# Grouped heads: two weight parts split in a head's first slot, the output's low part right behind the rotation, and fewer small VectorE instructions

## The chip, the cores and the metric

The kernel runs on one core of one Trainium2 chip. The metric is the device time of one execution in microseconds, the median of three runs. Five engines work side by side and meet at semaphores: TensorE (PE, matrix products and transposes), VectorE (DVE), ScalarE (ACT), GpSimd (POOL) and SyncE (SP, which issues the transfers).

## The reference, cut to what matters

The program computes two transformer blocks one after the other on 512 tokens of width 1024. The change touches one stage of the first, the differential attention of eight heads:

```python
def rms_norm(x, g):
    y = x * lax.rsqrt(jnp.mean(x*x, axis=-1, keepdims=True) + NORM_EPS)
    return y * g

def diff_attention(h, cos, sin, w_qkv, q_norm, k_norm, lam_p, subln, w_o, layer_idx):
    q, k, v = jnp.split(h @ w_qkv, [DA_QK, 2 * DA_QK], axis=-1)
    q = apply_rope(rms_norm(q.reshape(B, S, DA_HEADS, 2, HEAD_DIM), q_norm), cos, sin)
    k = apply_rope(rms_norm(k.reshape(B, S, DA_HEADS, 2, HEAD_DIM), k_norm), cos, sin)
    ...
    def one_block(args):                      # one block of 128 queries
        s = jnp.einsum('bqhcd,bkhcd->bhcqk', qblk, k) * scale
        p = jax.nn.softmax(jnp.where(causal, s, NEG_INF), axis=-1)
        a = p[:, :, 0] - lam * p[:, :, 1]
        return jnp.einsum('bhqk,bkhe->bqhe', a, v)
    ...
    o = rms_norm(o, subln) * (1.0 - lambda_init)
    return o.reshape(B, S, DA_V) @ w_o
```

A head has two score maps of depth 64 and one value matrix of width 128. Its two softmaxes are subtracted, and the result of each head is normalised over its 128 features. The rest of both blocks (grouped and windowed attention, convolutions, gated feed-forward layers, norms) is not touched.

## The kernel before

Every large product is made in three parts from operands split into a high and a low part: `w_hi` and `w_lo` for the weights, `hx_hi` and `hx_lo` for the activations. ACT writes `w_hi` from the loaded `w_raw`, and DVE writes `w_lo` as the difference.

**The stage of the heads** (`heads` on each engine) runs 8 heads, and each head `h` has 4 slots `i`, one for each block of 128 queries. The instructions of every engine stand in a fixed order, written by hand in its function `slot`; a head of the middle is one half of a loop body. In a slot, PE does in this order: the scores of head `h`, block `i` (L1991, with the mask at L1995); the transposes of the probabilities of the block before (L2004); in slot 3 the transposes of the output of head `h-1` (L2018, `turn_outputs`); the projection of one token tile of head `h+1`, 24 matmuls (L1969 to L1971); the product of the block before with the values (L2011); and `turn_qk`, the transposes of a rotated tile (L1979), which wait for DVE's `rope` of that tile. In slot 3, `turn_qk` shares a PSUM bank with the output of head `h-1` and waits for DVE's `outputs_low(h-1)` as well. PE takes its instructions in order, so whatever `turn_qk` waits for holds back the next slot.

DVE does in a slot: two row maxima of the scores (L1577); in slot 1 `outputs(h-1)` (L1540); in slot 2 `output_norm(h-1)` (L1550); `rope` (sum of squares L1489, mean L1491, rotation L1500, L1502, L1517, scaling L1520, which waits for POOL's root L523); `combine` (two reciprocals L1529 and L1530, the factor L1532, the difference of the probabilities L1535); in slot 1 `output_means(h-1)` (L1489 and L1491 again); in slots 1, 2 and 3 one `refill` (L1566), a third of `w_lo` for head `h+2`; and in slot 3 `outputs_low(h-1)` (L1555). ACT does the exponentials (L877), `weights` (L851), `output_squares` (L860), its half of the refill (L869), `outputs_high` (L856), the evacuation of the projection (L831, L834, L838) and `turned` (L843), the copy of what PE transposed.

**The weights of a head** come by one transfer of 1.5 MB into `w_raw[:, 0:3D]`, and there is one such buffer. SP issues the load for head `h+2` only when `w_lo` of head `h+1` is complete, which is at the end of `refill` in slot 3 of head `h-1`:

```python
with sp.Fori(2, nb) as i:
    load(st, 0, i, i + b0)        # waits until w_lo of head i-1 is complete
# ACT, refill:
if part == 0:
    act.wait_ge(s_loaded[0], 16 * (h + (st["loads0"][0] + 3)))
    act.wait_ge(s_mm, h + (st["block0"] + 1))
```

Heads 0 to 5 refill; heads 6 and 7 don't (`new=False`), and head 6 has splits of the next stage's weights (L675 on ACT, L1201 on DVE) after its slots 1 and 2. Head 7 projects nothing, and PE fills its slots with matmuls of the next stage (`pair`). The stage ends with PE's `turn(31, 3)`, a wait for `outputs_low(6)`, `pair(6, 7)`, the last product with the values, and then `outputs`, `output_means`, `output_norm` and `outputs_low` of head 7, one behind the other.

## Time and profile before

| what | us |
|---|---|
| median of 3 runs | 3028.74 (3027.15 to 3029.84) |
| the profiled execution, its own time | 3028.09 |
| its span, first to last instruction | 3026.3 |
| PE busy | 2786.0 (92%) |
| DVE busy | 1836.8 (61%) |
| ACT busy | 1080.0 (36%) |
| POOL busy | 118.8 (4%) |

The profile lists, for one execution, what each engine ran and when. Times of instructions are microseconds from the start of the span. A number in square brackets at the end of an instruction is the idle time of its engine just before it, and the instruction that released it. "PEclk" is the granted TensorE clock as a share of full speed; it shows two levels here, 1.00 (2.4 GHz) and 0.50 (1.2 GHz). The heads' stage is about a tenth of the span: the first scores stand at 46.4 us and the last low part of an output ends at 306.4 us.

### The profile page before, as it was taken

The page shows a single profiled execution, that of the slowest core. Times are in us where ns is not written, and L with a number is a line of the kernel's source. Part 1 is how long each engine was busy: PE and PEld are TensorE (multiplying, and loading weights), DVE is VectorE, ACT ScalarE, POOL GpSimd, SP SyncE. Part 2 cuts the span into 40 slices and gives each one's busy share as a digit, 9 for nine tenths or more (in the row PEclk, how much of TensorE's full clock was granted, in tenths as well). Part 3 has the DMA queues.
Part 4 walks back from the last instruction along what each step waited for, and adds up shares of the span by engine and source line. Part 5 has one row for each costly group of instructions (what it writes and reads, how often), then busy time and mean ns, then how long its engine had stood idle before and what let it go on. Part 6 is the DMA issues. An engine that isn't in the chain of part 4 may idle for free.

```text
span 3026.3 us, 41051 instructions
## 1 busy us (share of the span) xinstructions
PE 2786.0 (92%) x14220; PEld 2339.0 (77%) x14220; DVE 1836.8 (61%) x2910; ACT 1080.0 (36%) x1778; POOL 118.8 (4%) x148
## 2 busy tenths in 40 slices
PE   7999899997787999998986899999997899899998
PEld 6777788886676788887875788888886787688886
DVE  6766567676565577667996554353455455564645
ACT  5444332223565322223112232232223566352432
POOL 4111000000110000000000000000000000000000
PEclk8999999998898999998997999999998999999999
DMA  3111254452001355542110122122111000232321
GB/s 110 63 56 43 98 187 167 171 182 72 29 29 36 112 180 174 175 155 68 56 49 30 48 70 70 56 65 68 54 58 42 15 29 8 70 97 91 97 89 65
DMA packets 69314, 252.07 MB, mean 83 GB/s; under 512 B 7840, under 2 KB 10144, under 8 KB 66592
## 3 DMA queue, kind: packets, MB, share of 16 engines
q1 hardware_dynamic: 69152, 249.99, 24.5%
q8 instruction: 92, 1.51, 0.2%
q14 instruction: 70, 0.57, 0.1%
HBM read 247.87 MB, written 2.10 MB: 83 GB/s over the span
## 4 chain that ended last, share of the span: by engine, by line
PE 61%; DVE 16%; issue 15%; ACT 4%; DVEq 2%; POOLq 0%; ACTq 0%; POOL 0%; DMA 0%; SPq 0%
PE psum L1852 16%; PE psum L1851 16%; PE psum L1853 16%; DVE work L1372 4%; PE psum L2233 2%; DVE w_lo L1201 1%; ACT work L991 1%; PE psum L1991 1%; ACT sw_pt L1003 1%; PE psum L1969 1%; PE psum L1971 1%; PE psum L1970 1%; DVE neg_max L1740 1%; DVE tok_ms L1489 1%; DVE w_lo L1566 1%
## 5 line engine op out<-in xcount | busy, mean ns | idle before, releaser
L1851 PE MATMUL psum<-hx_hi,w_hi 128*128 128x512 f32 x1568 | 623.9, 398 | 28.9 <-DVE w_lo L1201 13.5
L1852 PE MATMUL psum<-hx_lo,w_hi 128*128 128x512 f32 x1568 | 625.1, 399 | 0.0
L1853 PE MATMUL psum<-hx_hi,w_lo 128*128 128x512 f32 x1568 | 623.7, 398 | 0.0
L675 ACT ACTIVATE w_hi<-w_raw 128x1024 fp32r<-128x1024 f32 (+1 forms) x328 | 344.6, 1051 | 527.2 <-PE psum L1853 231.4
L1201 DVE TENSOR_TENSOR w_lo<-w_raw,w_hi 128x1024 fp32r<-128x1024 f32 (+1 forms) x328 | 397.7, 1212 | 192.6 <-ACT w_hi L675 174.0
L1851 PEld LDWEIGHTS psum<-hx_hi,w_hi 128*128 128x128 f32 x1568 | 297.1, 189 | 79.1 <-issue 16.7
L1853 PEld LDWEIGHTS psum<-hx_hi,w_lo 128*128 128x128 f32 x1568 | 297.1, 189 | 69.9
L1852 PEld LDWEIGHTS psum<-hx_lo,w_hi 128*128 128x128 f32 x1568 | 298.0, 190 | 48.4
L1851 PE MATMUL psum<-a_hi,w_hi 128*128 128x512 f32 (+1 forms) x656 | 234.1, 357 | 18.1 <-DVE a_lo L1313 10.0
L1852 PE MATMUL psum<-a_lo,w_hi 128*128 128x512 f32 (+1 forms) x656 | 234.8, 358 | 0.0
L1853 PE MATMUL psum<-a_hi,w_lo 128*128 128x512 f32 (+1 forms) x656 | 233.9, 357 | 0.0
L1851 PE MATMUL psum<-o_hi,w_hi 128*128 128x512 f32 x544 | 217.8, 400 | 5.6 <-DVE o_lo L1778 3.9
L1852 PE MATMUL psum<-o_lo,w_hi 128*128 128x512 f32 x544 | 216.8, 398 | 0.0
L1853 PE MATMUL psum<-o_hi,w_lo 128*128 128x512 f32 x544 | 216.7, 398 | 0.0
L1335 DVE SCALAR_TENSOR_TENSOR work<-psum,vec,work 128x511 f32<-128x511 f32 (+1 forms) x132 | 83.2, 658 | 164.3 <-ACT work L758 156.3
L523 POOL TENSOR_TENSOR tok_r<-tok_ms,half 128x4 f32<-128x4 f32 (+1 forms) x70 | 71.8, 1025 | 2502.2 <-DVE tok_ms L1115 1949.6
L1277 DVE SCALAR_TENSOR_TENSOR X<-psum,mods,X 128x512 f32<-128x512 f32 x96 | 60.6, 658 | 178.6 <-PE psum L1853 177.1
L1851 PEld LDWEIGHTS psum<-a_hi,w_hi 128*128 128x128 f32 x656 | 125.2, 191 | 38.5 <-DVE a_lo L1313 10.5
L758 ACT ACTIVATE work<-psum,vec 128x768 f32<-128x768 f32 (+1 forms) x88 | 70.0, 795 | 223.5 <-PE psum L1853 215.8
L1852 PE MATMUL psum<-hc_lo,w_hi 128*128 128x256 f32 x512 | 144.8, 283 | 0.0
L1851 PE MATMUL psum<-hc_hi,w_hi 128*128 128x256 f32 x512 | 144.8, 283 | 0.0
L1853 PE MATMUL psum<-hc_hi,w_lo 128*128 128x256 f32 x512 | 144.5, 282 | 0.0
(289 smaller groups left out, 4914.2 us busy)
## 6 DMA issues: line engine op xcount, KB each, us to landing
mod_w<-in_w_mod SPq DMA_DIRECT2D x96, 512.0 KB, 3.6
w_raw<-in_fup SPq DMA_DIRECT2D x88, 512.0 KB, 4.5
w_raw<-in_cup SPq DMA_DIRECT2D x88, 512.0 KB, 3.5
w_raw<-in_fdown SPq DMA_DIRECT2D x32, 512.0 KB, 4.6
w_raw<-in_cdown SPq DMA_DIRECT2D x32, 512.0 KB, 3.5
w_raw<-in_da_qkv SPq DMA_DIRECT2D x6, 1536.0 KB, 6.5
w_raw<-in_fdown SPq DMA_DIRECT2D x16, 384.0 KB, 3.1
w_raw<-in_cdown SPq DMA_DIRECT2D x16, 384.0 KB, 3.0
```

The lines of the kernel that those rows point to most:

```text
L523: pool.tensor_tensor(tok_r[:, a:b], tok_ms[:, a:b], half[:, a:b], ALU.pow).then_inc(done, 1)
L675: r = act.activation(w_hi[:, off:off + n], w_raw[:, raw:raw + n], ACT.Copy)
L758: act.activation(wk[:, s, 0:toks], ps_of(st, s, 0, toks), ACT.Copy, scale=vec[:, bass.ds(b + col, 1)]).then_inc(s_ctap, 1)
L991: r = act.activation(work[:, e:e + (w1 - w0)], psum[:, w0:w1], ACT.Exp, bias=neg_max[:, col:col + 1], scale=root, accum_out=row_sum[:, col ...
L1201: r = dve.tensor_tensor(w_lo[:, off:off + n], w_raw[:, raw:raw + n], w_hi[:, off:off + n].bitcast(F32), ALU.subtract)
L1277: r = dve.scalar_tensor_tensor(X[:, b, a:e], ps_of(st, s, a, e), mods[:, l, c, bass.ds(b + o, 1)], X[:, b, a:e], ALU.mult, ALU.add)
L1335: dve.scalar_tensor_tensor(dst[:, a + 1:e], src(a, e - 1), prev, dst[:, a + 1:e], ALU.mult, ALU.add)
L1372: dve.scalar_tensor_tensor(acc, u[:, j:j + n], w, acc, ALU.mult, ALU.add)
L1851: pe.matmul(dst, wh, xh, start=first, stop=False)
L1852: pe.matmul(dst, wh, xl, start=False, stop=False)
L1853: return pe.matmul(dst, wl, xh, start=False, stop=last)
L2233: r = pe.matmul(pb[:, 5, 0:256], v_cols(tiles[k], g, p % 2), sw_pt[:, n % 2, 256 * i:256 * i + 256], start=p % 2 == 0 and k == 0, stop=p % ...
```

## The change

Seven things are done, all in the stage of the heads.

1. `refill`: parts 0 and 1 stand in slot 0 and part 2 in slot 3, instead of one part in each of the slots 1, 2 and 3. Head 0 keeps the old places.
2. DVE: `output_norm` stands behind `rope` in slot 2, and `outputs_low` behind `rope` and ahead of `combine` and `refill` in slot 3. On ACT `outputs_high` stands ahead of the refill.
3. `rope`: the mean (L1491) is gone. POOL's root takes the plain sum; the sum has a 65th column per head that holds 64 times epsilon, and the factors go into the gains. The drain behind the sum is gone with it. ACT writes the squares into `head_sq`, which is 65 columns apart.
4. `output_means` is gone from DVE. ACT takes the squares in four pieces of 128 columns with an accumulator each, in place of one of 512; POOL adds epsilon ahead of its root.
5. `combine`: one reciprocal of two columns in place of two.
6. `inv0` has a new shape, and `out_eps` is new.
7. The windowed attention of the later stages reads and writes `inv0` in its new shape.

```diff
-inv0 = sbuf("inv0", [P, 8])
+inv0 = sbuf("inv0", [P, 2, 4, 2])
+out_eps = sbuf("out_eps", [P, 4])
...
+head_sq = sw_vb[:, :, 0:4 * (HD + 1)].rearrange("p a (n f) -> p a n f", n=4)
...
+FIRST_REFILL, REFILL = ((), (0,), (1,), (2,)), ((0, 1), (), (), (2,))
...

+    def root_of_sum(a, b, ready, value, done):
+        pool.wait_ge(ready, value)
+        pool.tensor_tensor(tok_ms[:, a:b], tok_ms[:, a:b], out_eps[:], ALU.add)
+        pool.drain()
+        pool.tensor_tensor(tok_r[:, a:b], tok_ms[:, a:b], half[:, a:b], ALU.pow).then_inc(done, 1)
+
     def angles():
+        pool.memset(head_sq[:, :, :, HD:HD + 1], HD * EPS)
+        pool.memset(out_eps[:], P * EPS)
         pool.wait_ge(s_small, 32)
...
     def head_gains():
...
-        pool.tensor_scalar(g4[:, 0:128], gains_qk[:, 0:128], HD ** -0.5, None, ALU.mult)
-        pool.tensor_copy(g4[:, 128:256], gains_qk[:, 128:256])
+        pool.tensor_scalar(g4[:, 0:128], gains_qk[:, 0:128], 1.0, None, ALU.mult)
+        pool.tensor_scalar(g4[:, 128:256], gains_qk[:, 128:256], HD ** 0.5, None, ALU.mult)
...
-                        root(16, 20, s_da["oms"], h + 1, s_da["por"])
+                        root_of_sum(16, 20, s_da["osq"], h + 1, s_da["por"])
...
-            root(16, 20, s_da["oms"], 7, s_da["por"])
-            root(16, 20, s_da["oms"], 8, s_da["por"])
+            root_of_sum(16, 20, s_da["osq"], 7, s_da["por"])
+            root_of_sum(16, 20, s_da["osq"], 8, s_da["por"])
...
-                pool.tensor_copy(inv_wide[:], inv0[:, 0:4].unsqueeze(2).broadcast_to([P, 4, HD])).then_inc(S["invw"], 1)
+                pool.tensor_copy(inv_wide[:], inv0[:, 0, 0:2, :].rearrange("p a c -> p (a c)").unsqueeze(2).broadcast_to([P, 4, HD])).then_inc(S["invw"], 1)
...
-            act.activation(work[:, 2048 + 256 * (t % 2):2304 + 256 * (t % 2)], pb[:, bank, 0:256], ACT.Square,
-                           scale=root)
+            act.activation(head_sq[:, t % 2, :, 0:HD], pb[:, bank, 0:256].rearrange("p (n f) -> p n f", n=4),
+                           ACT.Square, scale=root)
...
         def output_squares(h):
...
-            act.activation(da_osq[:], da_osb[:].rearrange("p t e -> p (t e)"), ACT.Square)\
-               .then_inc(S["osq"], 1)
+            for t in range(4):
+                r = act.activation(da_osq[:, t * P:(t + 1) * P], da_osb[:, t, :], ACT.Square,
+                                   accum_out=tok_ms[:, 16 + t:17 + t])
+            r.then_inc(S["osq"], 1)
...
         def refill(h, par, part):
...
-            if i and new:
-                refill(h, par, i - 1)
...
+            if new:
+                for part in (FIRST_REFILL if first else REFILL)[i]:
+                    refill(h, par, part)
...
-            mean_squares(work[:, 2048 + 256 * (t % 2):2304 + 256 * (t % 2)].rearrange("p (n f) -> p n f", n=4),
-                         8 + 4 * (t % 2), 4, HD, S["rms"])
+            dve.tensor_reduce(tok_ms[:, 8 + 4 * (t % 2):12 + 4 * (t % 2)],
+                              head_sq[:, t % 2], AX, ALU.add).then_inc(S["rms"], 1)
...
-            dve.reciprocal(ratio[:, i:i + 1], row_sum[:, 2 * i + 1:2 * i + 2])
-            dve.reciprocal(inv0[:, 4 * par + i:4 * par + i + 1], row_sum[:, 2 * i:2 * i + 1])
-            dve.drain()
-            dve.scalar_tensor_tensor(ratio[:, i:i + 1], ratio[:, i:i + 1], row_sum[:, 2 * i:2 * i + 1],
+            dve.reciprocal(inv0[:, par, i, :], row_sum[:, 2 * i:2 * i + 2])
+            dve.drain()
+            dve.scalar_tensor_tensor(ratio[:, i:i + 1], inv0[:, par, i, 1:2], row_sum[:, 2 * i:2 * i + 1],
...
         def outputs(h, par):
...
-                              bc(inv0[:, 4 * par:4 * par + 4], P), ALU.mult).then_inc(S["osb"], 1)
-            dve.drain()
-
-        def output_means(h):
-            dve.wait_ge(S["osq"], h + 1)
-            mean_squares(da_osq[:].rearrange("p (t e) -> p t e", t=4), 16, 4, P, S["oms"])
+                              bc(inv0[:, par, :, 0], P), ALU.mult).then_inc(S["osb"], 1)
+            dve.drain()
...
         def output_norm(h):
...
                 outputs(h - 1, 1 - par)
-            if i == 2 and not first:
-                output_norm(h - 1)
             if i == 0:
...
                 rope(j + 3, i - 1)
-            combine(h, par, i)
-            if i == 1 and not first:
-                output_means(h - 1)
-            if i and new:
-                refill(h, par, i - 1)
+            if i == 2 and not first:
+                output_norm(h - 1)
             if i == 3 and not first:
                 outputs_low(h - 1)
+            combine(h, par, i)
+            if new:
+                for part in (FIRST_REFILL if first else REFILL)[i]:
+                    refill(h, par, part)

...
-        dve.tensor_scalar(sub_gain[:], vcol("subln"), 1.0 - LAMBDA_INIT, None, ALU.mult)
+        dve.tensor_scalar(sub_gain[:], vcol("subln"), (1.0 - LAMBDA_INIT) * math.sqrt(P), None, ALU.mult)
...
-        output_means(7)
...
-            dve.reciprocal(inv0[:, 0:4], sw_sum[:]).then_inc(S["inv"], 1)
+            dve.reciprocal(inv0[:, 0, 0:2, :].rearrange("p a c -> p (a c)"), sw_sum[:]).then_inc(S["inv"], 1)
...
         def outputs(m):
```

Where the instructions stand now is shown for three places. First VectorE from the end of slot 0 of a head to the first work of slot 1. `da_whi` counts the parts of `w_hi` that ACT has written, `da_sc` the scores, `da_av` the products with the values. Before:

```order
L1529 RECIPROCAL ratio<-row_sum 128x1 [waits da_ex]
L1530 RECIPROCAL inv<-row_sum 128x1
L1532 SCALAR_TENSOR_TENSOR ratio<-ratio,row_sum,neg_lam 128x1
L1535 SCALAR_TENSOR_TENSOR work<-work,ratio 128x128
L1576 REGISTER_ALU
L1577 TENSOR_REDUCE neg_max<-psum 128x1 [waits da_sc]
L1576 REGISTER_ALU
L1577 TENSOR_REDUCE neg_max<-psum 128x1 [waits da_sc]
L1540 TENSOR_TENSOR da_osb<-psum,inv 128x512 [waits da_av]
```

and in the changed kernel:

```order
L1543 RECIPROCAL inv<-row_sum 128x2 [waits da_ex]
L1545 SCALAR_TENSOR_TENSOR ratio<-inv,row_sum,neg_lam 128x1
L1548 SCALAR_TENSOR_TENSOR work<-work,ratio 128x128
L1572 ISA
L1575 TENSOR_TENSOR w_lo<-w_raw,w_hi 128x1024 [waits da_whi]
L1572 REGISTER_ALU
L1575 TENSOR_TENSOR w_lo<-w_raw,w_hi 128x1024 [waits da_whi]
L1585 REGISTER_ALU
L1586 TENSOR_REDUCE neg_max<-psum 128x1 [waits da_sc]
L1585 REGISTER_ALU
L1586 TENSOR_REDUCE neg_max<-psum 128x1 [waits da_sc]
L1553 TENSOR_TENSOR da_osb<-psum,inv 128x512 [waits da_av]
```

Two refills have come between the end of slot 0 and the maxima of slot 1. Second, ScalarE in slot 0 of a head, from the last `weights` to the evacuation of the projection. `raw_loaded0` is the arrival of the transfer. Before:

```order
L850 REGISTER_ALU [waits da_tra]
L851 ACTIVATE da_aT<-psum 128x512 [waits da_av]
L828 REGISTER_ALU
L831 ACTIVATE da_qk<-psum,tok_r 128x256 [waits da_pj]
L833 REGISTER_ALU
L834 ACTIVATE work<-psum,tok_r 128x256 [waits da_rms]
```

and in the changed kernel:

```order
L861 REGISTER_ALU [waits da_tra]
L862 ACTIVATE da_aT<-psum 128x512 [waits da_av]
L879 ISA
L880 REGISTER_ALU [waits raw_loaded0]
L882 ACTIVATE w_hi<-w_raw 128x1024 [waits block_multiplied]
L882 ACTIVATE w_hi<-w_raw 128x1024
L839 REGISTER_ALU
L842 ACTIVATE da_qk<-psum,tok_r 128x256 [waits da_pj]
```

The wait for the transfer and both halves of `w_hi` have come ahead of the evacuation. Third, VectorE at the end of slot 3, from the scaling of `rope` on. `w_hi_ready` is ACT's third part, `da_ohi` ACT's high part of the output. Before:

```order
L1520 TENSOR_TENSOR da_qk<-work,tok_r 128x256 [waits da_pr]
L1529 RECIPROCAL ratio<-row_sum 128x1 [waits da_ex]
L1530 RECIPROCAL inv<-row_sum 128x1
L1532 SCALAR_TENSOR_TENSOR ratio<-ratio,row_sum,neg_lam 128x1
L1535 SCALAR_TENSOR_TENSOR work<-work,ratio 128x512
L1565 REGISTER_ALU
L1566 TENSOR_TENSOR w_lo<-w_raw,w_hi 128x1024 [waits w_hi_ready]
L1555 ISA [waits da_ohi]
L1555 SCALAR_TENSOR_TENSOR o_lo<-psum,sub_gain,o_hi 128x512
```

and in the changed kernel:

```order
L1534 TENSOR_TENSOR da_qk<-work,tok_r 128x256 [waits da_pr]
L1564 ISA [waits da_ohi]
L1564 SCALAR_TENSOR_TENSOR o_lo<-psum,sub_gain,o_hi 128x512
L1543 RECIPROCAL inv<-row_sum 128x2 [waits da_ex]
L1545 SCALAR_TENSOR_TENSOR ratio<-inv,row_sum,neg_lam 128x1
L1548 SCALAR_TENSOR_TENSOR work<-work,ratio 128x512
L1574 REGISTER_ALU
L1575 TENSOR_TENSOR w_lo<-w_raw,w_hi 128x1024 [waits w_hi_ready]
```

The low part of the output now stands ahead of the combination and of the refill that completes `w_lo`.

## Rows read from the trace of the kernel before

**Rows 1.** Stretches: length; busy us of PE, PEld, DVE, ACT, POOL; PEclk; DMA share; GB/s.

```profile
85.78:253.23 167.45, 152.51 (x812) 127.42 (x811) 118.57 (x281) 79.65 (x206) 25.17 (x25) 0.95 0.16 57
178.60:182.00 3.40, 3.40 (x12) 3.40 (x11) 2.77 (x9) 0.80 (x3) 1.01 (x1) 0.50 0.60 253
267.40:270.70 3.30, 3.30 (x12) 2.14 (x11) 2.94 (x6) 1.47 (x5) 0.07 (x1) 0.50 0.39 112
```

**Rows 2.** Timeline, PE, one head: start, length, line, shape, [idle before, releaser].

```profile
151.06 0.70 PE L1991 MATMUL psum<-da_T 64*128 64x256 f32 x2
...
157.37 0.91 PE L1991 MATMUL psum<-da_T 64*128 64x384 f32 x2
...
165.42 0.44 PE L1979 MATMUL psum<-ident,da_qk 128*128 128x128 f32 x2 [1.14 <-DVE da_qk L1520]
165.79 1.12 PE L1991 MATMUL psum<-da_T 64*128 64x512 f32 x2
...
176.53 0.41 PE L1979 MATMUL psum<-ident,da_qk 128*128 128x128 f32 x2 [2.62 <-DVE o_lo L1555]
...
185.32 0.70 PE L1991 MATMUL psum<-da_T 64*128 64x256 f32 x2
```

**Rows 3.** Timeline, DVE, the same head, its slots 1 to 3.

```profile
153.34 0.69 DVE L1540 TENSOR_TENSOR da_osb<-psum,inv 128x512 f32<-128x512 f32 x1 [0.17 <-issue]
154.20 0.42 DVE L1489 TENSOR_REDUCE tok_ms<-work 128x4 f32<-128x256 f32 x1 [0.18 <-issue]
154.70 0.17 DVE L1491 TENSOR_SCALAR tok_ms<-tok_ms 128x4 f32<-128x4 f32 x1
154.97 0.46 DVE L1500 TENSOR_TENSOR work<-da_qk,da_tab_c 128x256 f32<-128x256 f32 x1
...
156.50 0.43 DVE L1520 TENSOR_TENSOR da_qk<-work,tok_r 128x256 f32<-128x256 f32 x1
...
157.61 0.48 DVE L1535 SCALAR_TENSOR_TENSOR work<-work,ratio 128x256 f32<-128x256 f32 x1
...
159.30 1.23 DVE L1566 TENSOR_TENSOR w_lo<-w_raw,w_hi 128x1024 fp32r<-128x1024 f32 x1 [0.17 <-issue]
160.68 1.02 DVE L1577 TENSOR_REDUCE neg_max<-psum 128x1 f32<-128x384 f32 x2
...
175.53 0.75 DVE L1555 SCALAR_TENSOR_TENSOR o_lo<-psum,sub_gain,o_hi 128x512 f32 x1 [0.33 <-issue]
```

**Rows 4.** Transfers of the heads' weights in the stretch 100 to 240 us.

```profile
w_raw<-in_da_qkv SPq DMA_DIRECT2D x4, 1536.0 KB, 6.5
```

**Rows 5.** Timeline, ACT, the same head.

```profile
154.06 0.63 ACT L860 ACTIVATE da_osq<-da_osb 128x512 f32<-128x512 f32 x1
...
170.64 1.07 ACT L869 ACTIVATE w_hi<-w_raw 128x1024 fp32r<-128x1024 f32 x1
...
178.46 0.37 ACT L877 ACTIVATE work<-psum,neg_max 128x128 f32<-128x128 f32 x1
...
178.81 0.59 ACT L851 ACTIVATE da_aT<-psum 128x512 f32<-128x512 f32 x1
```

**Rows 6.** Timeline, PE, head 0 (first row) and head 6 (second row).

```profile
50.79 0.69 PE L1979 MATMUL psum<-ident,da_qk 128*128 128x128 f32 x2 [3.19 <-DVE da_qk L1520]
...
265.35 0.44 PE L1979 MATMUL psum<-ident,da_qk 128*128 128x128 f32 x2 [1.09 <-DVE da_qk L1520]
```

**Rows 7.** Timeline, DVE, the last slot of head 7 and the stage's end.

```profile
295.75 0.75 DVE L1535 SCALAR_TENSOR_TENSOR work<-work,ratio 128x512 f32<-128x512 f32 x1
296.60 0.75 DVE L1555 SCALAR_TENSOR_TENSOR o_lo<-psum,sub_gain,o_hi 128x512 fp32r<-128x512 f32 x1
300.06 0.69 DVE L1540 TENSOR_TENSOR da_osb<-psum,inv 128x512 f32<-128x512 f32 x1 [2.71 <-PE psum L2011]
...
303.50 0.69 DVE L1550 TENSOR_TENSOR da_osb<-da_osb,tok_r 128x512 f32<-128x512 f32 x1 [1.12 <-POOL tok_r L523]
```

**Rows 8.** Timeline, ACT, the high part of head 6's output.

```profile
295.84 0.69 ACT L856 ACTIVATE o_hi<-psum,sub_gain 128x512 fp32r<-128x512 f32 x1
```

More of the change, by code:

```diff
@@ L311, in program @@
                  "pje", "qte", "ex", "ate", "osq", "ohi",
-                 "rms", "rope", "mx", "comb", "osb", "oms", "osc", "olo",
+                 "rms", "rope", "mx", "comb", "osb", "osc", "olo",
                  "pr", "por", "whi")
```

## The prediction, made before the changed kernel was run

> **What bounds the kernel now.** I read the timelines of PE, DVE and ACT side by side for one middle head, then the waits of PE, then the clock by stretches. All edits lie in the heads' stage, a tenth of the span, and only what ends later or earlier on PE there can move the time. In the head shown, PE takes 34.26 us from slot 1 of one head to slot 1 of the next (151.06 to 185.32) and stands still twice [rows 2]: 1.14 us in slot 2, since `rope` is late, and 2.62 us at the end of slot 3, since `turn_qk` waits for `outputs_low`. After the second wait the clock stood at half for 3.40 us [rows 1], which costs half of it, 1.7. So PE's own work is 34.26 - 1.14 - 2.62 - 1.7 = 28.8 us a head. The middle, heads 1 to 5, takes 167.45 us [rows 1]; 5 x 28.8 = 144.0 are work, and 23.4 are waits and half speed. That is all the change could win there.
>
> **The loop that the change makes.** Both waits of before are DVE being busy with refills while `rope` is due. Moved away, they go. But parts 0 and 1 now stand in slot 0, and their weights are asked for only when part 2 of the head before is done, at the end of slot 3. Before, ACT came to part 0 in slot 1, long after the arrival, so no row shows a wait for it. Now the transfer stands in a closed loop, which I add up from rows, from the end T of part 2:
>
> - The transfer is issued some 0.2 us behind T (an issue gap in the rows is 0.17, [rows 3]) and lands 6.5 us later [rows 4]: T + 6.7. ACT waits for it, with the evacuation of the projection queued behind.
> - ACT's part 0 takes 1.07 [rows 5], then DVE's two parts with their gaps 2 x 1.38 (159.30 to 160.68, [rows 3]): T + 10.5. ACT's part 1 hides behind DVE's part 0.
> - DVE goes on to slot 1: two maxima 0.9 (a pair of 384 columns takes 1.02, this one has 256), `outputs` 0.86 (153.34 to 154.20), `rope`. `rope` lasted 2.73 (154.20 to 156.93, [rows 3]). Without mean and drain, the 0.77 from the sum to the rotation (154.20 to 154.97) should become 0.35: the sum's own 0.42, less a small overlap, since nothing stands between the two any more (estimate 0.07). That saves 0.42 and leaves 2.31; with a gap left behind the sum it saves only the mean's own 0.27 (154.70 to 154.97). So `rope` ends at T + 14.6, and with the hand-over and the two transposes (0.1 and 0.37, [rows 2]) the scores of slot 2 start at T + 15.1.
> - Slot 2 is PE's alone: 165.79 - 157.37 - 1.14 = 7.28 [rows 2]. DVE has slack there now, with neither refill nor norm ahead of `rope`.
> - Slot 3, from the scores on: PE gives the second scores at 2.3 (two of 1.12 and a mask, [rows 2]), the second maximum ends at 3.1 (0.7 for 512 columns, estimated from 1.02 for two of 384, [rows 3]), `rope` from 3.3 to 5.6, `outputs_low` 0.75 and its gap of 0.33 to 6.7 [rows 3], `combine` 1.3 (the piece ahead of the difference 0.6, the difference 0.75, [rows 3, 7]) to 8.0, part 2 and gaps 1.4 to 9.4. ACT's high part is ready by then, since it stands ahead of the refill.
>
> The loop: 15.1 + 7.3 + 9.4 = **31.8 us**, against 28.8 of PE's work. So PE waits 3.0 us in slot 1 of heads 1 to 5, in one place, in place of 1.14 and 2.62. Bounds: 32.6 if `rope` saves 0.27 alone (twice 0.15) and the estimates of gaps and landing fall 0.5 short; 31.0 if they are 0.8 too long.
>
> **The clock.** The mean granted clock of the middle was 0.95 [rows 1]: twice 5% of 167.45 are 16.7 us at half speed, five stretches of 3.4, so about one a head, with two waits a head. A wait of 2.62 us was followed by a stretch of 3.40 us at 0.50, and one of 1.09 us in head 6 [rows 6], ahead of long scores, by 3.30 us [rows 1]. The wait of 3.0 us is longer than both, and the scores of slot 2 follow it. I take one such stretch in each of the five heads, 1.7 us each, on PE's path since slot 2 has no slack. The Trainium skill (TensorE: Matmul & The Clock Gate, HAM oscillation) tells of a loop in which the wait for a transfer lowers the clock in every round; it speaks against this change. [...]
>
> The middle: 5 x (31.8 + 1.7) = 167.5 us, against 167.45. **Nothing is won there: 0.0**, bounds -4 to +4 from the loop.
>
> **Around the middle.**
>
> - Head 0: PE waits 3.19 us for `rope` in slot 0 [rows 6], and `rope` is the bound in slot 1 too. Two times 0.42: **-0.8** (bounds 0 and -1.0).
> - Head 6 has no refill, so no loop. Its wait of 1.09 us in slot 2 [rows 6] goes: `output_norm` (0.8 with its gap, as long as `outputs`, [rows 3]) and 0.42 leave the way ahead of it. With it goes the stretch at half speed behind it, 3.30 us, so 1.7 [rows 1]: **-2.8** (bounds -1.1 and -2.8).
> - Head 7, slot 3: here `outputs_low` ahead of `combine` is a loss. ACT's high part runs from 295.84 to 296.53 [rows 8], and DVE's combination was over at 296.50 before it [rows 7]. Now DVE waits for ACT, does the low part to 297.35 and then `combine` (0.6 + 0.75): 298.7. PE's `turn(31, 3)` waits for this, and `pair` behind it could start once the low part was done, at 297.35 [rows 7] and a hand-over, 297.5; now at 298.7 + 0.1 + 0.4 = 299.2: **+1.7** (bounds +1.0 and +2.2).
> - The tail of head 7: the squares took 0.63 [rows 5]. A piece of 128 columns with an accumulator takes 0.35 (178.46 to 178.81, [rows 5]), four take 1.4, with the last reading 1.5: +0.9. The means go: 1.0 (between 158.09 and 159.30 they fill 1.04 beside a gap of 0.17, [rows 3]). POOL's addition has no row; it costs between a gap of 0.17 and 1.12, what its root took with the hand-over [rows 7]. I take 0.5, nearer to the low end for four columns. Sum **+0.4** (bounds 0 and +1.0). In heads 0 to 6 both are covered, by ACT's wait for the projection and by POOL's idle time.
> - `combine`'s reciprocal (no more than a part of the 0.68 between `rope` and the difference, [rows 3], and off PE's path but in slot 3), the shape of `inv0`, the set-up on POOL: 0. ACT's squares hide behind the projection in slot 1; if they did not, 0.9 a head.
>
> Sum: 0.0 - 0.8 - 2.8 + 1.7 + 0.4 = **-1.5 us**. The profiled execution took 3028.09 (its span 3026.3 and 1.8 around it), 0.65 below the median; the difference carries over: 3028.74 - 1.5 = **3027.2**.
>
> One rule weighs against my `rope`. The Trainium skill (VectorE: DVE Perf Modes, The DRAIN you can't avoid) says that the pipeline empties behind each operation, with or without a semaphore, so only the instruction would be saved. By it `rope` shrinks by 0.27, not 0.42, and the sum comes to +0.3 (0.15 at two places in each of five loops and twice in head 0, 1.8 in all). Two maxima behind each other, 1.02 for two of 384 columns [rows 3], are too near to either to decide; I keep 0.42.
>
> **Rivals.**
>
> - *The clock stays up.* The waits become one instead of two, and one place a head may pass unharmed. For it: of the two waits a head before, half passed without a stretch (five stretches, ten waits). Then 5 x 1.7 less: 3018.7. Chance 0.20.
> - *The weights come in time.* If the loop has slack (an earlier issue, a shorter slot 3), PE runs through: 144.0 in the middle, 23.5 less: 3003.7. Against it: 6.5 us of landing stand in the rows. Chance 0.06.
> - *Slower: a second stretch at half speed in each head.* The wait of 3.0 us is split by a short product, and behind it stand the scores of slot 2, with little for PE in them. If the clock is down twice in a row, each head pays 1.7 more: 5 x 1.7 = 8.5, 3035.7. It decides from three such heads on. Chance 0.12.
> - *The code does not do it:* the order shows each move in place, so what remains is that drains save nothing, above.
>
> **How the numbers follow.** The forecast, between 3022 and 3033 by its bounds, 0.62; the rivals 0.20, 0.06 and 0.12. The range reaches over the first rival and leaves the other two out: 3017 to 3034. A measurement of this kernel tells about 0.2%, 6 us, from no change. Faster by more: both gaining rivals and a little of the forecast's edge, 0.29. Slower by more: 0.11. Within: 0.60.
>
> **What would show it.** In the profile after: ACT idle before its first `w_hi` part in slot 0, released by the transfer, up to 4 us; a wait of PE near 3 us at `turn_qk` of slot 1, for `rope`; none in slots 2 and 3; DVE's sum to rotation 0.35 apart; one stretch at 0.50 in slot 2 of heads 1 to 5; the middle (between `outputs` of heads 0 and 5) near 167 us; `outputs_low` in front of `combine` at head 7 with PE's wait behind it. I am wrong if ACT does not wait for the transfer, or if the clock stays up.

## The result, and the profile after

The changed kernel took **3040.2 us** in the median (3039.2 to 3042.0), the kernel before 3029.1 in the same session (3027.2 to 3030.6): ratio 1.0038, 95% interval 1.0025 to 1.0051. It is slower by 11 us, where 3027.2 was forecast and 3034 was the upper end. The profiled execution took 3041.98 us (span 3040.2), 13.9 more than that of before.

Where the 13.9 us lie, by the same marks in both traces (the starts of DVE's scaling of the outputs, one a head, then the last low part, then the end):

| stretch | before | after | difference | forecast |
|---|---|---|---|---|
| start to first mark | 85.78 | 86.31 | +0.5 | -0.8 |
| the middle, five heads | 167.45 | 171.59 | +4.1 | 0.0 |
| head 6 | 30.46 | 27.62 | -2.8 | -2.8 |
| head 7 up to its last output | 16.37 | 19.61 | +3.2 | +1.7 |
| tail of the stage | 6.34 | 6.83 | +0.5 | +0.4 |
| everything behind the heads | 2719.9 | 2728.2 | +8.3 | 0 |

The marks of the first two rows need a correction. In the changed kernel the scaling of the outputs stands on DVE behind the two refills of slot 0, which wait for the transfer, so in heads 1 to 5 the mark comes 5.1 to 6.8 us after PE's first scores of slot 1; in head 6, which refills nothing, it comes 2.2 after them, as in the heads of before (2.2 to 2.3). The first mark is held up and the last of the middle is not. PE's own scores of slot 1, of head 1 and of head 6, before and then after:

```profile
83.50 0.70 PE L1991 MATMUL psum<-da_T 64*128 64x256 f32 x2
...
251.03 0.70 PE L1991 MATMUL psum<-da_T 64*128 64x256 f32 x2
```

```profile
81.19 0.70 PE L1998 MATMUL psum<-da_T 64*128 64x256 f32 x2
...
255.70 0.70 PE L1998 MATMUL psum<-da_T 64*128 64x256 f32 x2
```

On PE, then, the start is 2.3 us shorter, the middle has 174.5 us instead of 167.5, which is 7.0 more, and the other rows stay as they are.

The stretches of after that answer to [rows 1]: length; busy us of PE, PEld, DVE, ACT, POOL with instruction counts; PEclk; DMA share; GB/s. The first is the middle, then one stretch inside head 4's slot 2, and one in head 7:

```profile
86.31:257.90 171.59, 158.34 (x795) 127.97 (x794) 104.83 (x228) 79.24 (x241) 29.15 (x30) 0.89 0.15 56
...
196.00:202.60 6.60, 6.60 (x18) 4.27 (x18) 3.64 (x9) 2.00 (x6) 1.59 (x2) 0.50 0.00 0
...
301.90:305.00 3.10, 3.10 (x12) 2.60 (x10) 0.00 (x0) 0.02 (x1) 0.00 (x0) 0.50 0.00 0
```

The mean granted clock of the middle fell from 0.95 to 0.89, and one stretch at half speed is 6.6 us long where before it was 3.4. Such a stretch stands in each of the five heads, 6.6 to 6.8 us long in four of them and 10 in head 2, whose two waits were 1.82 and 1.77 us (124.5 to 134.5). That is 37 us at half speed in all, against 17 before.

One head of after, engine by engine, as in [rows 2, 3]. First the issue of the transfer (SP's queue), then ACT's part 0 and 1 of the refill, then DVE, then PE:

```profile
181.09 0.33 SPq L471 DMA_DIRECT2D w_raw<-in_da_qkv  x1
```

```profile
187.81 2.01 ACT L882 ACTIVATE w_hi<-w_raw 128x1024 fp32r<-128x1024 f32 x2 [5.07 <-DMA w_raw<-in_da_qkv]
```

```profile
179.69 1.23 DVE L1575 TENSOR_TENSOR w_lo<-w_raw,w_hi 128x1024 fp32r<-128x1024 f32 x1 [0.16 <-issue]
...
188.90 2.60 DVE L1575 TENSOR_TENSOR w_lo<-w_raw,w_hi 128x1024 fp32r<-128x1024 f32 x2 [3.88 <-ACT w_hi L882]
191.64 0.76 DVE L1586 TENSOR_REDUCE neg_max<-psum 128x1 f32<-128x256 f32 x2
192.49 0.69 DVE L1553 TENSOR_TENSOR da_osb<-psum,inv 128x512 f32<-128x512 f32 x1
193.35 0.42 DVE L1528 TENSOR_REDUCE tok_ms<-sw_vb 128x4 f32<-128x260 f32 x1 [0.17 <-issue]
193.69 0.42 DVE L1514 TENSOR_TENSOR work<-da_qk,da_tab_c 128x256 f32<-128x256 f32 x1
...
195.18 0.42 DVE L1534 TENSOR_TENSOR da_qk<-work,tok_r 128x256 f32<-128x256 f32 x1
...
214.33 1.22 DVE L1575 TENSOR_TENSOR w_lo<-w_raw,w_hi 128x1024 fp32r<-128x1024 f32 x1 [0.17 <-issue]
```

```profile
193.43 0.46 PE L2018 MATMUL psum<-da_v,da_aT 128*128 128x128 f32 x2 [0.86 <-ACT da_aT L862]
195.66 0.48 PE L1986 MATMUL psum<-ident,da_qk 128*128 128x128 f32 x2 [1.77 <-DVE da_qk L1534]
196.06 1.65 PE L1998 MATMUL psum<-da_T 64*128 64x384 f32 x2
...
206.16 1.12 PE L1998 MATMUL psum<-da_T 64*128 64x512 f32 x2
```

The loop stands there as it was summed. From the end of part 2, T = 180.92, the issue is 0.2 later, ACT starts at T + 6.9, DVE's two parts end at T + 10.6, `rope` ends at T + 14.7, and the scores of slot 2 start at T + 15.1, which is the predicted figure. Slot 3 begins at 206.16, and the next T is 215.55: 9.4 us, as predicted. Between them lies slot 2, and it takes 10.1 us instead of 7.28. The whole turn is 34.6 us, against 31.8 + 1.7 in the forecast.

### The profile page after: what moved, and what is told of

It reads as the page before. It is cut to its first block, busy times and chain, and to the rows that moved or that the text cites. A ratio compares the mean times of both kernels' runs of the same rounds, so it can differ in the third digit from the quotient of the medians.

```text
span 3040.2 us, 40964 instructions
## 1 busy us (share of the span) xinstructions
PE 2804.3 (92%) x14220; PEld 2345.8 (77%) x14220; DVE 1819.1 (60%) x2830; ACT 1083.9 (36%) x1834; POOL 124.1 (4%) x158
## 4 chain that ended last, share of the span: by engine, by line
PE 61%; issue 16%; DVE 14%; ACT 4%; DVEq 2%; DMA 1%; POOLq 0%; POOL 0%; ACTq 0%; SPq 0%
PE psum L1860 16%; PE psum L1858 16%; PE psum L1859 16%; DVE work L1386 4%; PE psum L2240 2%; PE psum L1998 1%; DVE w_lo L1215 1%; ACT work L1005 1%; DMA w_raw<-in_da_qkv 1%; ACT sw_pt L1017 1%; PE psum L1976 1%; PE psum L1977 1%; PE psum L1978 1%; DVE w_lo L1575 1%; DVE neg_max L1747 1%
## 5 line engine op out<-in xcount | busy, mean ns | idle before, releaser
L1858 PEld LDWEIGHTS psum<-a_hi,w_hi 128*128 128x128 f32 x656 | 125.0, 191 | 37.2 <-DVE a_lo L1327 10.4
```

The costliest lines, as they stand in the source:

```text
L1858: pe.matmul(dst, wh, xh, start=first, stop=False)
```

## The experiments

Three questions were open: whether the loop is the cause, what the clock has to do with it, and why the stages behind the heads, which the change hardly touches, had become 8.3 us longer. A fourth came up on the way: what the other parts of the change are worth without the moved refills. Times are medians; the kernel before had 3027.7 to 3029.1 us in the sessions of these runs, and ratios are against it.

### Cutting the transfer in two

The parts that slot 0 needs are requested as soon as DVE has split part 1, a head earlier; part 2 follows from slot 3.

```diff
-with sp.Fori(2, nb) as i:
-    load(st, 0, i, i + b0)
+def load_parts(i):
+    sp.dma_start(w_raw[:, 0:2 * D], dram["da_qkv"][i, :, 0:2 * D]).then_inc(s_loaded[0], 16)
+    sp.wait_ge(s_lo, i + b0)
+    sp.dma_start(w_raw[:, 2 * D:3 * D], dram["da_qkv"][i, :, 2 * D:3 * D]).then_inc(s_da["ld2"], 16)
+sp.wait_ge(s_lo, 2 + b0)
+load_parts(2)
+with sp.Fori(3, nb) as i:
+    sp.wait_ge(s_da["wf"], i - 2)        # DVE has split part 1
+    load_parts(i)
...
+if part == 2:                            # ScalarE, ahead of part 2
+    act.wait_ge(S["ld2"], 16 * (h + 1))
...
+if part == 1:                            # VectorE, behind part 1
+    r.then_inc(S["wf"], 1)
```

> The changed kernel with the load of a head's raw weights cut in two: parts 0 and 1 are requested as soon as VectorE has split part 1 (slot 0), part 2 as soon as it has split part 2 (slot 3). The refill of slot 0 then finds its weights a whole head early, and the closed loop (end of part 2's refill, transfer, two refills, rope, slot 3) is cut. Loop theory with the clock: PE's waits of 1.8 us twice in slot 1 of heads 1 to 5 go (3.5 us each), and the half-speed stretches of 3.4 us, two in each head, go with them (3.0 us each): the middle of five heads falls from 171.6 to about 144 to 150 us, the time from 3040 to 3012 to 3020 us. Rival L1 (VectorE's two refills in slot 0, 2.7 us in one piece, hold up slot 1 even when the weights are there): waits of 1 to 3 us stay, 3028 to 3036. Rival L2 (the transfer was not what the loop hung on): 3040 within 2.

Measured: **3009.6 us**, ratio 0.9922 (0.9909 to 0.9936), 30.6 below the changed kernel and 2 below the expected stretch; its five runs lie between 3001.9 and 3012.1. Its middle:

```profile
85.41:227.67 142.26, 142.26 (x811) 120.02 (x811) 105.01 (x228) 79.88 (x241) 29.13 (x30) 1.00 0.20 67
```

PE is busy for the whole of the middle, without a wait, and the clock is at 1.00. The same order of instructions, with only the transfer earlier, takes 29.3 us less there, or 32.1 on PE's own marks (142.4 against 174.5). So the loop through the transfer was the cause, and DVE's two refills in a row (rival L1) hold nothing up.

### Filling the waits with products

```diff
+def fill(n):
+    for k in range(n):
+        pe.matmul(pb[:, 6, :], hx_hi[:, k, 0:P], hx_hi[:, k, :], start=True, stop=True)
...
+filled = i == 1 and more and not first
+if filled:
+    pe.wait_ge(S["qte"], j + 3)
+    fill(7)
 if not (first and i == 0):
...
     values(j - 1, par if i else 1 - par, (i - 1) % 4)
...
 elif more:
+    if filled:
+        fill(7)
     turn_qk(j + 3, i - 1)
```

> The changed kernel with products whose result nobody reads put in front of TensorE's two waits in slot 1 of heads 1 to 6: seven of 128x512 before the values of the tile before, seven before the transposes of q and k (about 1.6 us each time at full clock, less than the wait of 1.8 us that is there). Clock theory: the half-speed stretches behind slot 1 come from the idle time in it, so with it filled slot 2 of heads 1 to 5 falls from 10.2 to about 7.3 us and the time by about 3.0 x 5 = 15 us to 3025 us; head 6, which has no wait, gains nothing and may lose up to 3 us by the added products. Rival C1 (the clock is held down by the short products of the scores that follow, whatever stood before): slot 2 stays at 10.2 us and the time at 3040 or above. Rival C2 (the added products run at half speed and push the transposes out): 3045 or more.

Measured: **3029.1 us**, 11.1 below the changed kernel, where some 15 were expected; ratio to before 0.9999 (0.9990 to 1.0008). The middle and head 6:

```profile
87.29:243.95 156.66, 156.38 (x867) 130.26 (x866) 104.83 (x228) 79.26 (x241) 29.17 (x30) 1.00 0.17 61
243.95:274.73 30.78, 30.48 (x164) 24.61 (x163) 20.22 (x46) 14.51 (x45) 5.84 (x6) 1.00 0.11 35
```

PE does more work here than in the changed kernel, and the middle is 14.9 us shorter. Seven added products took 1.6 to 1.7 us at each place, together somewhat more than the waits of 2.6 that they fill, and PE has no wait left: what went away is the half speed. In head 6, where no wait was there to fill, they cost the 3.2 us that they last (30.78 against 27.62). So the clock theory holds. It shows best in slot 2, from its scores to those of slot 3: the five take 51.3 us in the changed kernel and 35.3 here, 3.2 less in each. Of the 32.1 us that the loop cost PE in the middle, 13.2 are PE standing still and 16.0 are these slots; the other 2.9 lie in the slots 1, where the clock is partly down too. Half of the 37 us at half speed is 18, so the clock is the larger part.

### Addresses: 64 bytes

The kernel before, with an unused tensor behind `inv0`:

```diff
 inv0 = sbuf("inv0", [P, 8])
+gap64 = sbuf("gap64", [P, 16])
```

> The kernel before with an unused tensor of 64 bytes per partition behind inv0, so that all that lies behind inv0 in SBUF (the activations hx, hc and a, and the heads' and sliding window's tensors) moves by 64 bytes as it does in the changed kernel; nothing else differs. Theory S (the shift of 64 bytes slows the stages behind the heads): the changed kernel's trace is 8.3 us longer behind the heads' stage, 5.3 of them in the feed-forward stage over 768 tokens (572.2 to 577.5 us), so this kernel should take 3029 + 6 to 8 = 3035 to 3037 us, its heads' stage end as before (306 us), and that feed-forward stage take about 577.5 us. Rival (the shift is nothing, the 8.3 us are chance of one execution or come from what the heads' stage leaves behind): 3029 us within 2, and 572.2 us for that stage.

Measured: **3036.7 us**, ratio 1.0022 (1.0013 to 1.0031): 7.6 us for 64 bytes that nobody touches. And the changed kernel with its new small tensors put where they move nothing:

```diff
+inv0 = small[:, 0:16].rearrange("p (a i c) -> p a i c", a=2, i=4)   # small: allocated, unused
+out_eps = small[:, 16:20]
...
-inv0 = sbuf("inv0", [P, 2, 4, 2])
-out_eps = sbuf("out_eps", [P, 4])
+gap32 = sbuf("gap32", [P, 8])
```

> The changed kernel with inv0 and out_eps put into an existing unused tensor, and 32 bytes kept in their old place, so that every other tensor has the address it has in the kernel before; the instructions are the same. Theory S: the feed-forward stage over 768 tokens falls back from 577.5 to 572.2 us, the time from 3040 to about 3032 to 3034 us; the heads' stage stays at its 311.96 us. Rival: 3040 within 2, the stage at 577.5.

Measured: **3033.5 us**, ratio 1.0010 (1.0001 to 1.0019), against 1.0038 for the changed kernel. The feed-forward stage over 768 tokens, one row each of the kernel before, the changed one, before with 64 bytes, and the changed one with the old addresses:

```profile
1714.62:2286.80 572.18, 562.43 (x3192) 491.58 (x3192) 276.58 (x376) 161.92 (x178) 1.32 (x1) 0.99 0.19 60
```

```profile
1722.22:2299.74 577.52, 567.82 (x3192) 493.29 (x3192) 276.61 (x376) 161.99 (x178) 1.33 (x2) 0.98 0.18 60
```

```profile
1719.04:2296.61 577.57, 567.88 (x3192) 493.31 (x3192) 276.61 (x376) 161.91 (x178) 1.32 (x2) 0.98 0.19 60
```

```profile
1722.42:2294.58 572.16, 562.41 (x3192) 490.87 (x3192) 276.62 (x376) 161.94 (x178) 1.32 (x1) 0.99 0.19 60
```

The same 3192 matmuls take 5.4 us more of PE's time with the activations, and all else behind `inv0`, moved by 64 bytes. The clock (0.99 and 0.98 here) is not the reason: in the long run at 1.00, eight rounds of six matmuls take 8.40 us before and 8.48 after, and there are 528 such rounds. Before, then after:

```profile
2270.27 0.39 PE L1851 MATMUL psum<-a_hi,w_hi 128*128 128x512 f32 x1
...
2278.67 0.39 PE L1851 MATMUL psum<-a_hi,w_hi 128*128 128x512 f32 x1
```

```profile
2282.79 0.40 PE L1858 MATMUL psum<-a_hi,w_hi 128*128 128x512 f32 x1
...
2291.27 0.40 PE L1858 MATMUL psum<-a_hi,w_hi 128*128 128x512 f32 x1
```

It repeats in every kernel of this study: this stage took 572.16 to 572.19 us in the six with the old addresses and 577.3 to 577.9 in the seven with the moved ones, whatever else they did. The stage behind it has about 1 us more (344.6 to 345.0 against 345.2 to 346.3). The rest of the 8.3, some 2 us, did not go by the address: the first feed-forward stage took 387.5 or about 389 in kernels of both kinds, and what makes that difference was not found.

A third place was tried, 96 bytes on (`gap96`, 24 columns):

> The kernel before with 96 unused bytes per partition behind inv0, so that the tensors behind it start at a multiple of 128 bytes (32 beyond one before, 96 beyond one in the changed kernel). Theory D (what counts is the place within 128 bytes, and 96 beyond a multiple is a bad one): 3028 within 3 us, the feed-forward stage over 768 tokens 572 us or less. Theory E (any move from the old place costs, because the old place suits the other operand, which has not moved): that stage 577 us or more, 3034 to 3038. Theory F (the activations' start at a multiple of 128 bytes is best): less than 572 us in that stage and 3020 to 3026.

Measured: **3027.8 us**, ratio 0.9999 (0.9990 to 1.0008). The stage took

```profile
1712.95:2287.61 574.66, 564.88 (x3192) 492.98 (x3192) 276.63 (x376) 161.90 (x178) 1.32 (x1) 0.99 0.19 60
```

2.5 us more than in the old place, while the first feed-forward stage took 385.9, 1.6 less than before, and the total is that of before. None of the three theories fits alone: not every move costs as much, and a start at a multiple of 128 bytes is not the best for this stage. What in the address matters stays open.

### The refills back in slots 1, 2 and 3

```diff
-FIRST_REFILL, REFILL = ((), (0,), (1,), (2,)), ((0, 1), (), (), (2,))
+FIRST_REFILL, REFILL = ((), (0,), (1,), (2,)), ((), (0,), (1,), (2,))
```

> The changed kernel with the three refills of weights in slots 1, 2 and 3 of each head, as before; all other parts of the change stay. Loop theory: with the first refill in slot 1, a whole slot (some 7 us) lies between the request of the transfer and its first use, so the transfer of 6.5 us is hidden, the waits in slot 1 go, and with the output's low part ahead of the combination the waits of slot 3 in the kernel before (9.4 us for o_lo in five heads) stay away too: the middle of five heads takes 144 to 156 us instead of 171.6, the time is 3040 - 16 to 27 = 3013 to 3024 us. Rival (the loss comes from the other parts of the change, say ScalarE's four squares in slot 1 or the order in slots 2 and 3): the middle stays near 168 to 172 us, 3036 to 3040.

Measured: **3008.8 us**, ratio 0.9934 (0.9917 to 0.9950), a little below the expected stretch. The middle:

```profile
84.03:226.32 142.29, 142.29 (x812) 120.05 (x811) 107.29 (x230) 81.65 (x241) 29.14 (x30) 1.00 0.19 67
```

So one line of the change costs some 30 us, and all the rest of it gains 19 against the kernel before, the 64 bytes and head 7 paid. The first mark stands at 84.03 here, 1.75 before that of the kernel before.

### Only the move

The kernel before with the refills moved to slots 0 and 3, on DVE and on ACT. One thing more is in it: on ACT the refill of slot 3 now stands behind `outputs_high`, as in change 2, so it is not the move alone:

```diff
+FIRST_REFILL, REFILL = ((), (0,), (1,), (2,)), ((0, 1), (), (), (2,))
...
-if i and new:                            # ScalarE
-    refill(h, par, i - 1)
 if i == 3 and not first:
     outputs_high(h - 1)
+if new:
+    for part in (FIRST_REFILL if first else REFILL)[i]:
+        refill(h, par, part)
...
-if i and new:                            # VectorE
-    refill(h, par, i - 1)
+if new:
+    for part in (FIRST_REFILL if first else REFILL)[i]:
+        refill(h, par, part)
 if i == 3 and not first:
     outputs_low(h - 1)
```

> The kernel before with two of the three refills moved to slot 0 and nothing else changed (no shift of addresses, the output's low part behind the combination as before). Loop theory: the closed loop is there as in the changed kernel, with a rope that is 0.42 us longer, so the middle takes 171 to 175 us (before 167.5), head 6 loses its wait in slot 2 (-2.8), head 7 is as before: 3029 + 4 to 8 - 3 = 3030 to 3034 us, with waits in slot 1 of heads 1 to 5 of some 3 us each. Rival (the refill's move is free and the loss comes from the rest): 3026 to 3029.

Measured: **3031.0 us**, ratio 1.0009 (0.9999 to 1.0019), so a loss of 3 us that the interval hardly tells from none. The time was in the expected stretch, and so is the middle on PE's own marks: 171.2 us (83.70 to 254.89) against 167.5 before. DVE's marks hide this, as above. The mechanism was not the expected one. Stretch of the middle by DVE's marks, and PE's waits in it (waited for; us in total, times, longest):

```profile
89.56:257.09 167.53, 153.80 (x791) 128.20 (x791) 116.65 (x279) 78.74 (x206) 25.19 (x25) 0.91 0.16 57
```

```profile
PE psum L1982 <- DVE o_lo L1557: 10.3, 5, 2.4
PE psum L1982 <- DVE da_qk L1522: 2.3, 1, 2.3
```

The waits stand in slot 3, for the output's low part, as in the kernel before, and only two of them in slot 1 (the second row, and one of 0.8 us for `da_aT`). In the old order the low part comes behind T, so that PE is held up while the transfer runs, and when slot 1 comes, the weights are there. The same waits in the changed kernel's middle:

```profile
PE psum L1986 <- DVE da_qk L1534: 8.9, 5, 1.8
PE psum L2018 <- ACT da_aT L862: 4.3, 4, 1.8
```

There the order has removed the wait of slot 3, and the transfer has nothing left to hide behind. The two edits are each other's trap. In the middle, on PE's marks, the new order alone gains 14 us (below), the move costs 4, and the changed kernel, which has both and the fewer small instructions, costs 7.

### The new order alone, and the small instructions alone

`order_only` is the kernel before with change 2, but for head 7, which keeps its old order: scaling and low part behind the rotation on DVE, the high part ahead of the refill on ACT.

```diff
+if i == 3 and not first:                 # ScalarE
+    outputs_high(h - 1)
 if i and new:
     refill(h, par, i - 1)
-if i == 3 and not first:
-    outputs_high(h - 1)
...
-if i == 2 and not first:
-    output_norm(h - 1)
 if i == 0:
     rope(j + 3, 3)
 elif more:
     rope(j + 3, i - 1)
+if i == 2 and not first:
+    output_norm(h - 1)
+if i == 3 and not first and more:
+    outputs_low(h - 1)
 combine(h, par, i)
...
-if i == 3 and not first:
+if i == 3 and not first and not more:
     outputs_low(h - 1)
```

`small_only` is the changed kernel with the refills in their old slots and this order undone, so that the smaller count of small instructions and the 64 bytes are left:

```diff
-FIRST_REFILL, REFILL = ((), (0,), (1,), (2,)), ((0, 1), (), (), (2,))
+FIRST_REFILL, REFILL = ((), (0,), (1,), (2,)), ((), (0,), (1,), (2,))
...
+if i == 2 and not first:
+    output_norm(h - 1)
 if i == 0:
     rope(j + 3, 3)
...
-if i == 2 and not first:
-    output_norm(h - 1)
-if i == 3 and not first:
-    outputs_low(h - 1)
 combine(h, par, i)
...
+if i == 3 and not first:
+    outputs_low(h - 1)
```

> The kernel before with only the order of the heads' parts changed: ScalarE's o_hi ahead of its refill in slot 3, VectorE's scaling of the outputs (slot 2) and their low part (slot 3, not in head 7) right behind the rotation and ahead of the combination. Refills in slots 1 to 3, small instructions and addresses as before. Theory O (of the change, this order alone takes the waits of slot 3 away: 9.4 us for o_lo and 5.2 for da_qk in five heads, and with them the half speed): the middle falls from 167.5 to 143 to 148 us, head 6 by 2.8, the time from 3028 to 3001 to 3007 us. Rival (the order does it only with the shorter rope, since the rope's 2.73 us stand ahead of the low part now): waits of 0.4 to 1 us stay in slot 3, the clock falls, 3012 to 3024.

> The changed kernel with refill slots and the order of VectorE and ScalarE in the heads as before: what is left of the change is the smaller count of small instructions (sums of squares by ScalarE, one reciprocal for two) and the 64 bytes. Theory O: the waits for o_lo stay nearly (each 0.42 us shorter), half the clock loss stays: 3018 to 3034 us, the 64 bytes (+7) in it. Rival (the small instructions free VectorE enough to remove the waits by themselves): 3008 to 3012, as with the new order.

Measured: `order_only` **3010.3 us**, ratio 0.9934 (0.9919 to 0.9949); `small_only` **3016.1 us**, ratio 0.9953 (0.9938 to 0.9968). The middle of each, `order_only` first, and what is left of PE's waits:

```profile
86.24:239.26 153.02, 146.00 (x812) 120.80 (x811) 118.12 (x281) 78.73 (x206) 25.16 (x25) 1.00 0.17 62
```

```profile
PE psum L1971 <- DVE w_lo L1566: 3.5, 5, 1.1
PE psum L1981 <- DVE o_lo L1555: 1.9, 4, 0.5
PE psum L1981 <- DVE da_qk L1520: 1.3, 4, 0.4
```

```profile
83.75:237.77 154.02, 146.47 (x812) 123.23 (x811) 107.75 (x231) 83.08 (x241) 29.17 (x30) 0.98 0.17 62
```

```profile
PE psum L1986 <- DVE o_lo L1564: 7.3, 5, 1.5
```

Both times lie between the two theories on record. I expected the order to do nearly all and the small instructions little. Each alone takes 13 to 14 us out of the middle, and both together 25 (142.3). In neither do the waits vanish. For comparison, those of the kernel before over the same stretch:

```profile
PE psum L1979 <- DVE o_lo L1555: 9.4, 5, 2.6
PE psum L1979 <- DVE da_qk L1520: 5.2, 5, 1.1
```

Measured against the 142.3 of `old_slots`, `order_only` has 10.7 us too many with 6.7 of waits, `small_only` 11.7 with 7.3, and the kernel before 25.2 with 14.6. What is not wait is 4, 4.4 and 10.6. Of the 10.6, half speed explains 8.4 (half of 16.8 us). Shortening the waits by half took the half speed nearly away with them; the clock is back at 1.00 and 0.98. The 4.0 of `order_only` are therefore not the clock, and what they are was not looked into.

### Head 7

```diff
-if i == 3 and not first:
+if i == 3 and not first and more:
     outputs_low(h - 1)
 combine(h, par, i)
+if i == 3 and not more:
+    outputs_low(h - 1)
```

> The changed kernel, but in head 7, where no rope stands ahead, the output's low part behind the combination in slot 3, as before. Theory (VectorE waits 2.25 us for ScalarE's o_hi there, the combination and all behind it come late, and the clock falls for the last products of the head): the stretch between the last two output scalings falls from 19.6 to 16.4 us, the time from 3040 to about 3037 us. Rival (the low part is late anyway and the consumer behind it waits instead): 19.6 stays or the tail grows by as much, 3040.

Measured: **3037.6 us**, ratio 1.0031 (1.0018 to 1.0043), 2.6 below the changed kernel. Against the kernel before of its own session it has 9.8 us more, where the changed one had 11.1, and the two intervals overlap, so the whole time does not show the gain. The stretch does: up to the last output it fell from 19.61 to 16.40 us, with the clock at 1.00:

```profile
284.74:301.14 16.40, 15.61 (x74) 10.34 (x73) 7.65 (x16) 6.96 (x23) 1.21 (x2) 1.00 0.01 1
```

### Put together

Both versions join edits shown above: the addresses as in `nopad` and head 7 as in `old_head7`. `best1` adds the load in two pieces of `split_load`, `best2` the refills in slots 1 to 3 of `old_slots`.

> The changed kernel with the load cut in two, every address as before, and head 7's order as before. If the effects found so far (the loop -30, the addresses -7, head 7 -3) add up: 3009.6 - 7 - 3 = 2999 to 3003 us, the middle 142.3 us at full clock. Rival (they overlap, since the clock's falls lie elsewhere when the marks move): 3005 to 3010.

> The changed kernel with the refills in slots 1 to 3 as before, the load in one piece, every address as before, and head 7's order as before. If the terms add up: 3008.8 - 7 (addresses) - 1.8 (head 7: 18.1 to 16.3 us) = 2999 to 3001, the same as with the load cut in two, since the middle runs at full clock without a wait in both (142.3 us). If the cut load has a gain of its own: 3003 or more here.

Measured: `best1` **3000.6 us**, ratio 0.9908 (0.9892 to 0.9925); `best2` **2997.0 us**, ratio 0.9900 (0.9884 to 0.9915). Both beat both kernels. The terms add up within 2 us (`best2` was expected at 2999 to 3001), and the two intervals overlap, so the cut load shows no gain of its own: where the transfer is hidden anyway, hiding it better brings nothing. The middle of `best2`, then heads 6 and 7 up to the last output:

```profile
83.19:225.71 142.52, 142.52 (x812) 120.30 (x811) 107.30 (x231) 81.72 (x241) 29.17 (x30) 1.00 0.19 67
225.71:269.66 43.95, 42.85 (x223) 32.39 (x221) 27.87 (x61) 21.35 (x67) 7.03 (x8) 1.00 0.08 25
```

PE is busy for 142.52 of 142.52 us: the middle can only be made shorter by taking work off PE.

## Why the prediction was wrong, point by point

- **The loop, 31.8 us.** Right, in the whole and in its parts: T + 6.9, 10.6, 14.7, 15.1 against the predicted 6.7, 10.5, 14.6, 15.1, and 9.4 for slot 3. PE's waits are 0.86 + 1.77 = 2.6 in this head, 3.0 were forecast. They stand in slot 1, in two pieces, and there are none in slots 2 and 3. That the wait would be one, in one place, was wrong.
- **The clock, 1.7 us a head.** This is the term that failed in the middle. `fill_products` gives 16.0 us for the slots 2 of the five heads, 3.2 each, not far from twice the 1.7 that I took from one stretch of 3.40 us [rows 1], and the 37 us at half speed give 3.7 each. The rival with the second stretch was the right one; it stood at 0.12. What spoke for it was in the text: behind the longest wait yet, PE is to do short products with little in them. I sized the stretch by the one row of before, whose wait stood ahead of slot 0's products and projection, not ahead of slot 2's.
- **The middle, 0.0.** Measured +7.0 on PE, 174.5 us (+4.1 by DVE's marks). PE's own work was put at 144.0, and it is 142.4 (`split_load`, the same marks); the waits of the five heads' slots 1 sum to 13.2 (8.9 + 4.3), forecast 15.0; the rest, 174.5 - 142.4 - 13.2 = 18.9, is in the main the clock, forecast 8.5. Two errors of 1.6 and 1.8 helped, and one of 10.4 hurt.
- **Head 0, -0.8.** The first mark shows +0.5, but it lies behind the first refill of two parts, and the wait for the transfer is in it. On PE the gain is there, and larger: the scores of slot 3 started at 68.77 before and start at 66.50 now (before, then after),

```profile
68.77 1.12 PE L1991 MATMUL psum<-da_T 64*128 64x512 f32 x2
```

```profile
66.50 1.12 PE L1998 MATMUL psum<-da_T 64*128 64x512 f32 x2
```

  and those of slot 1 of head 1 are 2.3 earlier as well. Not all of it belongs to the change. In the five kernels with the old small instructions these scores of slot 3 start at 67.3 to 69.2, in the nine with the new ones at 66.2 to 68.4; the means are 1.3 apart, so a single pair proves little to 1 us.
- **Head 6, -2.8.** Right: 30.46 to 27.62, with the clock up and no wait in slot 2.
- **Head 7, +1.7.** Measured +3.2. The chain of waits is right: DVE waits for ACT's high part, then does the low part, then the combination, and PE waits for it:

```profile
298.45 0.75 DVE L1564 SCALAR_TENSOR_TENSOR o_lo<-psum,sub_gain,o_hi 128x512 fp32r<-128x512 f32 x1 [2.25 <-ACT o_hi L867]
...
299.82 0.75 DVE L1548 SCALAR_TENSOR_TENSOR work<-work,ratio 128x512 f32<-128x512 f32 x1
```

```profile
300.63 0.66 PE L2011 MATMUL psum<-ident,work 128*128 128x128 f32 x4 [1.86 <-DVE work L1548]
```

  The combination ends at 300.57, which is 298.74 on the clock of before (head 7's first mark is 1.83 later), against the predicted 298.7. What was left out is that this new wait of 1.86 us is followed by 3.1 us at half speed (the third row of the stretches above), 1.55 us. It is the same omission as in the middle: a new wait of PE was priced without the clock.
- **The tail, +0.4.** Measured +0.5. POOL's addition took 0.20.
- **The shape of `inv0`, 0.** Wrong, and next to the clock the largest term of the whole miss of 15.4 us (forecast -1.5, measured +13.9 in the traces). Of the 8.3 us behind the heads, 5.3 in one stage and about 1 in the next are shown to go by the address; 2 are not. I had looked at the tensors for what they compute and not for where they push the others.
- **`rope`, 0.42 saved.** Right: the rotation starts 0.34 after the start of the sum (193.35 to 193.69), before the sum's own 0.42 are over. The Trainium skill (VectorE: DVE Perf Modes, The DRAIN you can't avoid) would have the pipeline empty first; here it does not, and the run agrees instead with that section's remark that an operation which is not held starts earlier. The sum goes by the row.
- The Trainium skill's HAM oscillation (TensorE: Matmul & The Clock Gate) tells of a wait for a transfer in every turn, with the lower clock paid every time. The runs bear it out with 3.2 us in slot 2 of each of five heads; PE's own waits in it were 1.85 us at most, in four of the heads two behind each other.

Slower by over 0.2% had been given 0.11. With the clock's second stretch (-1.5 + 8.5 = +7.0) and the 64 bytes (+7.6, `pad64`) the sum would have been 3028.7 + 14.6 = 3043.3, with 3040.2 measured. That this is near is partly luck: PE's work, the waits and head 0 came out 4.9 us below their terms, the clock above even the doubled one.

## What to carry to other kernels

Before a step that needs loaded data is moved forward, follow the buffer around: if its transfer is requested at the end of the same round, the move closes a loop, and a wait that used to look wasteful elsewhere may have been its cover. A new wait of TensorE is priced twice, by its length and by the lower clock behind it, and a wait of 1.8 us ahead of short products can cost as much again and more. Shortening all waits to 1.1 us and less brought the clock back here, but the length of one wait does not decide. When small tensors change size, keep the addresses of the operands behind them, or time the kernel before with the same shift as a control.

## What the runs showed of the hardware

- The rate of a long run of fp32r matmuls depends on addresses in SBUF; what moved here are the activations, their moving operand, with all the small tensors behind `inv0`, and not the weights. A shift of 64 bytes made 3192 matmuls slower by 5.4 us (562.4 to 567.9 busy), with the same instructions; the stage's length went by this address in all fourteen kernels. 96 bytes made them slower by 2.5. I had not expected any effect.
- The granted clock stays at 1.00 through five heads with waits of up to 1.1 us (`order_only`), has 0.98 with waits of up to 1.5 (`small_only`), and goes to 0.89 with two of 0.7 to 1.8 us close to each other (the changed kernel). Products that nobody reads, put into the waits, bring it back to 1.00. No length of a wait alone explains it: in the kernel before, a wait of 1.07 us (to 132.26) was followed by 3.4 us at half speed, and one of 1.91 us (to 243.79) by none. What else decides stays open.
- DVE starts an operation 0.34 us after the start of a sum of 0.42 us when nothing stands between the two.
